# First halves of the merged tiles turned by VectorE blocks and a trip through memory instead of TensorE transposes

## The reference

```
for i, (y, g0) in enumerate(zip(ys, (COL_GA, COL_GB, COL_GC))):
    gated = y * jax.nn.silu(z[..., g0:g0 + BR_WIDTH])
    sel = jax.nn.sigmoid(z[..., COL_MG + i * D_MODEL:COL_MG + (i + 1) * D_MODEL])
    term = sel * (gated @ wb[i])
    out = term if out is None else out + term
return out @ wo
```

## Time and profile before

| | us |
|---|---|
| median of three runs | 1889.93 |
| all three | 1887.77, 1889.93, 1892.88 |
| the profiled execution | 1888.2 |
| its span | 1886.0 |
| TensorE busy in the span | 1861.1 (99%) |
| VectorE busy | 1343.8 (71%) |
| ScalarE busy | 1004.4 (53%) |

### The profile page before, as it was taken

The page is one execution under the profiler, slowest core; times in us unless marked ns, Lnnn a source line. Parts: engine busy times, 40 slices in busy tenths (PEclk is TensorE's granted clock), DMA queues, the critical chain, the costliest instruction groups (busy, mean ns, idle before and its releaser), DMA issues.

```text
span 1886.0 us, 26216 instructions
## 1 busy us (share of the span) xinstructions
PE 1861.1 (99%) x10592; PEld 1579.9 (84%) x10592; DVE 1343.8 (71%) x1832; ACT 1004.4 (53%) x1462; POOL 39.0 (2%) x47
## 2 busy tenths in 40 slices
PE   7999999999999999999999999999999999999998
PEld 3899888999888999988788887788888888778887
DVE  5798789898789888855655566755566555786555
ACT  3465544565544666544544466554455444665444
POOL 1300000000000000000000000000000000000000
PEclk8999999999999999999999999999999999999999
DMA  9565675665675666465477754377765777436775
GB/s 366 221 199 196 216 239 198 193 206 205 213 239 197 214 205 186 157 222 188 157 229 222 223 186 143 124 223 229 221 198 189 223 226 230 160 110 205 225 228 168
DMA packets 143672, 385.67 MB, mean 204 GB/s; under 512 B 24192, under 2 KB 50944, under 8 KB 142784
## 3 DMA queue, kind: packets, MB, share of 16 engines
q1 hardware_dynamic: 138672, 362.60, 59.0%
q0 software_dynamic: 4592, 19.90, 3.0%
q10 hardware_dynamic: 288, 1.51, 0.2%
HBM read 366.11 MB, written 15.73 MB: 202 GB/s over the span
## 4 chain that ended last, share of the span: by engine, by line
PE 89%; DVE 7%; ACT 1%; DMA 1%; issue 1%; SPq 0%; DVEq 0%; ACTq 0%
PE PS L707 27%; PE PS L709 27%; PE PS L708 27%; DVE w_lo L2136 2%; DMA raw<-weights 1%; PE PS L881 1%; PE PS L1284 1%; PE PS L892 1%; PE PS L985 1%; DVE arena L2346 1%; PE PS L1273 1%; PE PS L965 1%; ACT w_hi L1532 1%; PE PS L1117 0%; PE PS L869 0%
## 5 line engine op out<-in xcount | busy, mean ns | idle before, releaser
L2136 DVE TENSOR_TENSOR w_lo<-raw,w_hi 128x1024 fp32r<-128x1024 f32 x600 | 731.3, 1232 | 401.0 <-ACT w_hi L1532 399.7
L1532 ACT ACTIVATE w_hi<-raw 128x1024 fp32r<-128x1024 f32 x600 | 625.8, 1057 | 462.8 <-DMA raw<-weights 460.1
L707 PE MATMUL PS<-w_hi,h_hi 128*128 128x512 f32 (+1 forms) x1280 | 494.8, 387 | 2.2 <-DVE w_lo L2136 1.3
L709 PE MATMUL PS<-w_hi,h_lo 128*128 128x512 f32 (+1 forms) x1280 | 488.4, 382 | 0.0
L708 PE MATMUL PS<-w_lo,h_hi 128*128 128x512 f32 (+1 forms) x1280 | 488.0, 381 | 0.0
L707 PEld LDWEIGHTS PS<-w_hi,h_hi 128*128 128x128 f32 x1280 | 240.7, 188 | 54.8 <-issue 5.4
L709 PEld LDWEIGHTS PS<-w_hi,h_lo 128*128 128x128 f32 x1280 | 240.7, 188 | 46.8
L708 PEld LDWEIGHTS PS<-w_lo,h_hi 128*128 128x128 f32 x1280 | 240.8, 188 | 45.7 <-issue 1.0
L707 PE MATMUL PS<-h_hi,w_hi 128*128 128x256 f32 x896 | 257.8, 288 | 0.4 <-DVE h_lo L2515 0.2
L707 PE MATMUL PS<-w_hi,g_hi 128*128 128x512 f32 (+1 forms) x656 | 256.6, 391 | 0.4 <-DVE w_lo L2136 0.4
L708 PE MATMUL PS<-h_lo,w_hi 128*128 128x256 f32 x896 | 253.4, 283 | 0.0
(11 more groups left out here) (302 smaller groups left out, 1655.9 us busy)
## 6 DMA issues: line engine op xcount, KB each, us to landing
raw<-weights SPq DMA_DIRECT2D x610, 512.0 KB, 4.0
act_mem<-arena SPq DMA_DIRECT2D x144, 64.0 KB, 3.0
arena<-act_mem SPq DMA_DIRECT2D x36, 256.0 KB, 3.6
qk<-weights POOLq DMA_DIRECT2D x12, 512.0 KB, 5.1
v<-weights POOLq DMA_DIRECT2D x12, 512.0 KB, 4.0
x<-weights SPq DMA_DIRECT2D x8, 512.0 KB, 8.1
mix_mem<-arena SPq DMA_DIRECT2D x64, 64.0 KB, 1.8
arena<-mix_mem SPq DMA_DIRECT2D x16, 256.0 KB, 3.9
```

What stands on the lines that cost most here:

```text
L707: pe.matmul(dst, hi, m_hi_, start=first, stop=False, **kw)
L709: return pe.matmul(dst, lo, m_hi_, start=False, stop=last, **kw)
L1532: nc.scalar.activation(w_hi[:, r, :], raw[:, r, :], ACT.Copy).then_inc(w_hi_ready, 1)
L2136: V.tensor_tensor(w_lo[:, r, :], raw[:, r, :], f32(w_hi[:, r, :]), ALU.subtract).then_inc(w_lo_ready, 1)
```

## The change

In all three passes the two `turn_merged` calls for half 0 go from TensorE, and with them TensorE's wait for `m_lo` in group 4. VectorE turns `merged[:, t, 0, :]` by 32 x 32 blocks at the start of its part of group 3, ahead of the next splits. SyncE stores each tile with four DMAs and loads it back with one, behind the loads of slots that it issues while TensorE is in group 3. ScalarE and VectorE read the tile in SBUF in place of PSUM when they make its two parts in group 4, at the same place in their programs. The trips are numbered through with those of the attention (ten in a pass). Half 1 is turned as before.

```diff
@@ scratch
+        turned = scratch(5632, 1024).rearrange("p (t n) -> p t n", t=TT)
+        def trip(p, n):
+            return (HEADS_A * TT + TT) * p + n
+        def tile_trip(p, t):
+            return trip(p, HEADS_A * TT + t)
+        def of_blocks_t(t):
+            return turned[:, t, :].rearrange("p (i k e) -> p k i e", i=4, k=4)
@@ SyncE
+            def tile_out(p, t):
+                u = tile_trip(p, t)
+                sp.wait_ge(mix_blocks, u + 1)
+                sp.wait_ge(mix_moved[u % 2], 16 * (u // 2))
+                for i in range(4):
+                    rows = turned[32 * i:32 * i + 32, t, :].rearrange("p (j e) -> p j e", j=4)
+                    sp.dma_start(mix_mem[u % 2, :, :, i, :].rearrange("j a e -> a j e"), rows).then_inc(mix_stored, 16)
+            def tile_in(p, t):
+                u = tile_trip(p, t)
+                sp.wait_ge(mix_stored, 64 * (u + 1))
+                dst = turned[:, t, :].rearrange("p (i e) -> p i e", i=4)
+                sp.dma_start(dst, mix_mem[u % 2, :, :, :, :].rearrange("j a i e -> (j a) i e")).then_inc(mix_moved[u % 2], 16)
+            tile_moves = {start[f"pass{p}_merge"] + 18 + 1 + t + RING: (p, t) for p in range(3) for t in range(TT)}
+            tile_returns = {c + 1: m for c, m in tile_moves.items()}
...
+                if n in tile_returns:
+                    tile_in(*tile_returns[n])
+                if n in tile_moves:
+                    tile_out(*tile_moves[n])
@@ TensorE
-                if g == 4:
-                    pe.wait_ge(m_lo, 4 * p + 2)
...
-                if g == 3:
-                    turn_merged(p, 0, 0)
-                    turn_merged(p, 0, 1)
@@ ScalarE, merged_high
+                    if half == 0:
+                        u = tile_trip(p, t)
+                        act.wait_ge(mix_moved[u % 2], 16 * (u // 2 + 1))
+                        nc.scalar.activation(hi.rearrange("p k (i e) -> p k i e", i=4), of_blocks_t(t), ACT.Copy).then_inc(m_hi, 1)
+                        return
@@ VectorE
+                def turn_blocks(t):
+                    dve.wait_ge(merge_added, 8 * p + 2 + t + 1)
+                    V.transpose(turned[:, t, :].rearrange("p (j g e) -> p g j e", j=4, g=4),
+                                merged[:, t, 0, :].rearrange("p (g j e) -> p g j e", g=4, j=4)).then_inc(mix_blocks, 1)
...
+                    if g == 3:
+                        turn_blocks(0)
+                        turn_blocks(1)
                     for half in range(2):
                         for j in ((-1, 0, 1), (2, 3, 4))[half]:
                             split(c + j + AHEAD)
```

More of the change, by code:

```diff
@@ L583, in mix_out @@
             def mix_out(p, n):
-                u, nt = 8 * p + n, len(key_tiles(p))
+                u, nt = trip(p, n), len(key_tiles(p))
                 sp.wait_ge(mix_blocks, u + 1)
@@ L1033, in merge_group, with turn_merged @@
                         mm.then_inc(w_used, 1)
-                if g == 3:
-                    turn_merged(p, 0, 0)
-                    turn_merged(p, 0, 1)
-            def turn_merged(p, half, t):
-                pe.wait_ge(merge_added, 8 * p + 4 * half + 2 + t + 1)
+            def turn_merged(p, t):
+                pe.wait_ge(merge_added, 8 * p + 6 + t + 1)
                 for j in range(4):
                     mm = pe.transpose(PS[:, 6 + t, j * P:(j + 1) * P],
-                                      merged[:, t, half, j * P:(j + 1) * P], const("ident"))
+                                      merged[:, t, 1, j * P:(j + 1) * P], const("ident"))
                 mm.then_inc(m_turned, 1)
@@ L1063, in branch_sum @@
                 if j == 0:
-                    turn_merged(p, 1, 0)
+                    turn_merged(p, 0)
                     slot_ready(c)
                     merged_sum(p, c, dst[0], 0, True)
-                    turn_merged(p, 1, 1)
+                    turn_merged(p, 1)
                     slot_ready(c + 1)
@@ L1218, in last_sums @@
             def last_sums():
-                turn_merged(2, 1, 0)
+                turn_merged(2, 0)
                 out_slot(0, 0)
                 out_slot(0, 1)
-                turn_merged(2, 1, 1)
+                turn_merged(2, 1)
                 for i in range(1, 4):
@@ L1776, in merged_high @@
                 def merged_high(half, t):
-                    act.wait_ge(m_turned, 4 * p + 2 * half + t + 1)
-                    nc.scalar.activation(merged_half(p, half)[0][:, :, t * P:(t + 1) * P], of_token(t), ACT.Copy).then_inc(m_hi, 1)
+                    hi = merged_half(p, half)[0][:, :, t * P:(t + 1) * P]
+                    if half == 0:
[3 more added lines that the diff above has]
+                        return
+                    act.wait_ge(m_turned, TT * p + t + 1)
+                    nc.scalar.activation(hi, of_token(t), ACT.Copy).then_inc(m_hi, 1)
                 for g in range(6):
@@ L2514, in merged_low @@
                     hi, lo = (a[:, :, t * P:(t + 1) * P] for a in merged_half(p, half))
+                    if half == 0:
+                        V.tensor_tensor(lo.rearrange("p k (i e) -> p k i e", i=4), of_blocks_t(t),
+                                        f32(hi).rearrange("p k (i e) -> p k i e", i=4), ALU.subtract).then_inc(m_lo, 1)
+                        return
                     V.tensor_tensor(lo, of_token(t), f32(hi), ALU.subtract).then_inc(m_lo, 1)
+                def turn_blocks(t):
+                    dve.wait_ge(merge_added, 8 * p + 2 + t + 1)
+                    V.transpose(turned[:, t, :].rearrange("p (j g e) -> p g j e", j=4, g=4),
+                                merged[:, t, 0, :].rearrange("p (g j e) -> p g j e", g=4, j=4)).then_inc(mix_blocks, 1)
                 for g in range(6):
```

## The result

The changed kernel takes 1892.51 us (median of 20 runs, 1889.39 to 1899.34), the kernel before 1889.38 (20 runs). The ratio is 1.0017, 95% interval 1.001 to 1.0023: 3.1 us slower on the medians, between 1.9 and 4.3 by the interval. That lies inside the 0.3% forecast as no difference, but it is more than the 0.6 us of the sum, and clear of zero. The profiled execution took 1893.54 us, its span is 1891.4.

A forecast was written before the change was run, and what follows sets the result against it. TensorE, busy 1861.1 of 1886.0 us, was taken as the bound. Gain -2.6, VectorE's blocks +2.6 and group 4's sixth slot +0.6 made +0.6: 1888.8 profiled, 1890.4 on the median's level, range 1886.3 to 1895.5.

The forecast's parts named there:

- The gain, 2.6: Between groups 3 and 4, TensorE without its eight transposes saves 0.88 us a pass, 2.6 us in three passes.
- VectorE's blocks, 1.30 in passes 0 and 1: Two block transposes delay the split of group 3's third slot; TensorE waits 1.30 us more a pass, 2.6 together.
- Pass 2 hides them: At pass 2's third slot of group 3, slack of 1.2 us hides the two block transposes, keeping its 0.88.
- The third rival: Block transposes are on the path in pass 2 too: +1.9 us, 1891.8 on the median's level; chance 0.1.
- Nine microseconds of cover; the wait costs nothing.: Last tile returns near 269.7 in pass 0, ScalarE first wants it behind the split at 278.37: no cost.
- The sixth slot of group 4, 0.6 for both passes: In passes 0 and 1 TensorE wants this slot 0.88 earlier; 0.3 us a pass comes back as waiting.
- The second rival: Trips' traffic delays weight loads issued in group 3 of passes 0 and 1: +5.6 us, median level 1895.5; chance 0.2.
- The first rival: VectorE absorbs the two block transposes, only TensorE's 2.6 us go: 1887.3 on the median's level; chance 0.12.
- The Trainium skill's rule: Cited against moving half 0's transposes to VectorE: by it every pass would lose; the trace had 0.88 against 1.30.

The follow-up runs named there:

- the run without turning: Kernel before without TensorE's transposes of half 0 and nothing in their place: 1886.9 us, ratio 0.9995 to the kernel before.
- the run without them: Changed kernel with VectorE's blocks behind group 3's first split, without stores and returns of the tiles: 1885.5 us, ratio 0.9984 to the kernel before.
- behind one split: Changed kernel with VectorE's blocks behind group 3's first split, each return two slots behind its stores: 1896.7 us, ratio 1.0032 to the kernel before.
- the best version: Changed kernel, blocks behind group 3's first split, returns two slots behind stores, ScalarE's high parts ahead of group 4's fourth split: 1885.1 us, ratio 0.9975.
- the early parts: Kernel before with ScalarE's two high parts of half 0 ahead of group 4's fourth split: 1888.4 us, ratio 0.9993 to the kernel before.
- the late return: Changed kernel with each tile's return three slots behind its stores in place of one: 1889.4 us, ratio 1.0001 to the kernel before.

## Why the prediction was right, and where it was wrong

- **The forecast** was no difference that can be measured, 1890.4 (its terms add up to 1890.5). The time is 1892.5, inside the range, and slower by less than the 0.3%. The balance it rested on held in its first two terms and failed in the third. That the forecast came true owes as much to the width of 0.3%, 5.7 us, as to the balance: twenty runs of each kernel tell 3.1 us from nothing.
- **The gain, 2.6.** Right: 2.9 in the stretch of the run without turning, 0.97 of it in pass 2, and 2.7 on its medians, where the interval alone would allow none at all.
- **VectorE's blocks, 1.30 in passes 0 and 1.** Right: 1.19 each, and 2.0 us by themselves on the medians. The clue was the pair of the earlier trace rows: an engine back to back and TensorE idle at the end of it. Two took 1.22 (259.90 to 261.12).
- **Pass 2 hides them.** Right: its third slot has no wait. The third rival is out.
- **"Nine microseconds of cover; the wait costs nothing."** This step failed. For ScalarE it held, with some six us of cover in place of nine (issued at 272.67, about 3.9 to landing, wanted at 282.5). But the wait that counted was the other one, on SyncE: the prediction took the stores to land in 1.8, the median of the attention's, and looked for a wait at the first tile's return of pass 2 only. The second tile's stores landed 4.4 us after their last issue, with the DMA engines full in that time (share 1.03), and behind the return stood two loads of weights. With the return moved back, 2.2 us of the stretch went, the attention's wait not counted.
- **The sixth slot of group 4, 0.6 for both passes.** The place was right, the size too small. Against the run without turning, the way from the third slot of group 3 to the first slots of `wo` grew by 0.8 and 1.0 in passes 0 and 1, and pass 2 lost another 0.9 around its fourth slot, which the sum had at nothing: 2.7 in place of 0.6. Pass 2's part is in one trace only. Its reason was half right, too. The load does follow its release when there are no trips (4.5 to 5.1 us); with them it comes after 5.4 to 5.6 in the change, and after 4.4 to 8.1 in the runs that hang them elsewhere.
- **The second rival**, traffic that delays the weights, was given 0.2 and priced at +5.6. That trips delay a load on which TensorE then waits is real, as the run without them shows. The main place was wrong: nothing was lost at a slot behind the modulation rows of group 3, priced at 3.8, and everything at group 4's sixth slot and behind it, priced at 1.8. So was the price: behind one split the blocks cost nothing, and the trips cost 8 us of the stretch where the rival had 5.6 for all of them. That the run came out at +6.7, near the rival's +5.6, is chance. Whether VectorE's 1.2 us of delay masked a part of this in the change, by giving the transfers time, stays open: the run behind one split moves the returns too.
- **The first rival**, absorption on VectorE, is out.
- **The Trainium skill's rule** ("VectorE: DVE Perf Modes", section "Rules for kernel authors"), that TensorE should turn 128 x 128 tiles where PSUM may be the destination: the time of the change as made agrees with it, that of the best version doesn't. With the blocks off VectorE's critical moment and the high parts early, it is 4.9 us faster than before, of which the early parts by themselves may make 0.6 (stretch) to 1.6 (medians).

## What to carry to other kernels

Where an engine is 99% busy, price a piece of work moved off it by the moment at which it lands on the other engine, not by that engine's busy share: 1.2 us on a VectorE that is 71% busy cost all of it in one place, and nothing at that slot when they stood one split later. A queue that issues the weights must not wait for a round trip: hang the return far enough back that its wait is over, by the landing time of full DMA engines (4.4 us here) and not by the median (1.8). And before adding transfers, look for what hangs on a load by program order alone; two instructions moved ahead of one split were worth more here (3.9 us of the last column) than the late return (2.2).

## What the runs showed of the hardware

- Behind waits of TensorE of 2.81, 2.85 and 3.72 us the granted clock was 0.50, the 1.2 GHz level: the matmuls stood 0.43 us apart in place of 0.23 for two to three microseconds. Behind the waits of 1.54 and 1.56 us it stayed at 1.00.
- In windows of 4 to 6 us the DMA engines' share was full (0.99 to 1.06) at 319 to 399 GB/s, with the weights, the modulation loads and the trips together. A load of 512 KB then took up to 8.1 us, against a median of 4.0.
- Removing a short wait made a following one longer: the run behind one split has 0.35 in place of 1.54 at the third slot of group 3, 2.81 in place of 0.96 at the sixth of group 4, and was the slowest.
